# Two edits of order in the second input projection: the fifth normed tile and the sums of the second half

## The chip, the cores and the metric

The kernel runs on one core of one Trainium2 chip. The metric is the device time of one execution in microseconds (us), the median of a few runs. Weights and activations are float32; a product is made as three matmuls of a rounded part and its remainder (hi x hi, hi x lo, lo x hi), which is why TensorE is busy nearly all the time.

## The reference, cut to what matters

Two transformer blocks in a row, 1024 tokens, width 1024. Between them stand the places that the change touches:

```python
    # end of the first block
    gate = sigmoid(rmsnorm(h, ln3_g) @ w_ple_gate)
    h = h + gate * (p @ w_ple_proj)             # the "ple" stage
    h = rmsnorm(h, lnf_g)
    # start of the second block
    x = layer_norm(h, ln_in_g, ln_in_b)
    proj = x @ w_in_2                           # the second input projection, 22 column tiles of 128
```

The two norms are made as one: with d = lnf_g * h, the layer norm of the RMS norm needs the sum of d, the sum of d squared and the sum of h squared over the 1024 features of each token.

## The kernel before, in words

Data lie feature-major: tile k of h is 128 features (partitions) x 1024 tokens, k = 0 to 7. A half n is 512 tokens. All five engines run a list of instructions written out by hand; they meet at semaphores only, and each engine works through its own list in strict order, so an instruction that waits holds up everything behind it on that engine.

**The last four ple columns** are made as eight pieces, `PIECES` (line 83): pieces 0 to 3 are columns 4 to 7 of half 0, pieces 4 to 7 the same columns of half 1. PE's `piece` (line 1149) makes 24 matmuls for one. VectorE then does for each piece j: `piece_read` (line 2602, out of PSUM), `piece_gated` (2609, times the projected p, after ScalarE's sigmoid), `piece_added` (2616, into h), `piece_centre` (2622, d = lnf_g * h less a shift, after ScalarE has squared h), `sq1(j, 0)` and `sq1(j, 1)` (line 2678, which call `piece_square_in`, 2629: adding ScalarE's squares of h and of d). The plain sum of d is added by GpSimd's `piece_sum` (713) or, for pieces 3 and 7, by VectorE's `piece_sum_in` (2639).

**The norm of a half** goes: PE's `half_sums` (line 1179; 16 small matmuls, line 1175, that add over the partitions), VectorE's `half_variance` (2646; three small instructions), ScalarE's `half_root` (1850), VectorE's `half_inverse` (2655) and `half_factors` (2660), PE's `half_rows` (1210; 16 small matmuls, line 1217, that spread the two factors over the partitions into PSUM). VectorE's `normed` (2665) then makes each tile k of that half with a multiply (line 2672) and a subtraction (line 2676), both of SBUF with PSUM. ScalarE's `normed_hi` (1855) applies gain and offset (line 1858) and rounds to `B_hi` (line 1864); GpSimd's `normed_lo` (720) makes the remainder `B_lo` (line 726).

**The projection's first four columns** are made by PE's `quad` (line 1270). For a half n it loops over the eight tiles k, and for each k over four columns j, in four PSUM banks: eight matmuls from `B_hi` (lines 1259 and 1262) and four from `B_lo` (line 1266). It waits for `op_hi` of tile k ahead of the eight and for `op_lo` ahead of the four. What stands in the dictionary `before` is issued ahead of tile k and of its wait.

So `quad(0, ...)` runs on the normed tiles of half 0 while the last ple pieces of half 1 are still being finished on VectorE, and the sums and rows of half 1 are issued between its tiles.

**ScalarE's list** in this stretch (lines 1887 to 1893) stays as it is:

```python
            normed_hi(0, 0), piece_square(6, 0), normed_hi(1, 0), piece_gate(7)
            normed_hi(2, 0), piece_square(6, 1), normed_hi(3, 0), piece_square(7, 0), normed_hi(4, 0), piece_square(7, 1), normed_hi(5, 0)
            tick(act.activation(R[0:1, 0:1], col("one")[0:1, :], ACT.Sqrt))
            half_root(N1, 1, "ln_rms_eps")
            normed_hi(6, 0)
            tick(act.activation(R[0:1, 0:1], col("one")[0:1, :], ACT.Sigmoid))
            normed_hi(7, 0)
```

`piece_square(7, 0)` waits for `piece_added(7)`, `piece_square(7, 1)` for `piece_centre(7)`. `piece_centre(7)` overwrites h and waits for `piece_square(7, 0)`. GpSimd's list (lines 742 and 743) is `normed_lo` of tiles 0, 1 and 2, `piece_sum(6)`, `normed_lo` of tiles 3 to 7, and then the second half. It stays too.

Of the kernel before, what the change touches and what calls it, by code (L numbers as in the profile page):

```python
# [86 lines left out]
N1 = Norm(S_PLE, C_PLE, E3 + 2 * FULL, 2, FULL, 5, 0, 4, 0, 3, 2, 0)  # L87
# [97 lines left out]
def build(nc, x_t, p_t, weights, vec, w_gate_up, consts, masks, onehot, window, rel_bias, w_sp, rows, b_sp, bias_scratch,  # L185
          out):
    with ExitStack() as ctx:
# [8 lines left out]
        def at(name, kb, shape, dt=F32):  # L196
            return nc.alloc_sbuf_tensor_at(name, shape, dt, offset=base + int(kb * KB))
# [68 lines left out]
        acc2 = at("acc2", 40, [P, T])  # L266
# [122 lines left out]
        def hs(n):  # L389
            return slice(n * HT, (n + 1) * HT)  # L390
# [32 lines left out]
        def col(name, j=0):  # L423
            return vecs[:, bass.ds(VEC[name] + j, 1)]
# [32 lines left out]
        def quad(t, m, n):  # L457
            return t[:, m, n * HT:(n + 1) * HT]
# [360 lines left out]
        def _(pe):  # L819
# [352 lines left out]
            def sums_by_quarter(st, n, which, src, start=True, stop=True):  # L1172

                for g in range(4):
                    mm = pe.matmul(sums_of_half(st, n, which)[g * QP:(g + 1) * QP, :], ones[:, 0:QP], src[:, g * P:(g + 1) * P],
                                   start=start, stop=stop)
                return mm

            def half_sums(st, n, total, last=True):


                if n and st is N2:
                    pe.wait_ge(acc_free[1], (st.out + KT - 2) // 2 + 1)
                elif n == 0:
                    pe.wait_ge(pc_read, st.made + 3)
                pieces = 4 * n + (4 if last else 3)
                if not last:
                    pe.wait_ge(pc_read, st.made + 4)
                pe.wait_ge(sum_done, st.sq + st.per * pieces)
                pe.wait_ge(part_done, st.part + pieces)  # L1190
                sums_by_quarter(st, n, 0, acc[:, hs(n)], stop=last)
                mm = sums_by_quarter(st, n, 1, total[:, hs(n)], stop=last)
                if last:
                    mm.then_inc(stat_done, 1)
# [15 lines left out]
            def half_rows(st, n):  # L1210

                pe.wait_ge(hf_small, st.small + 5 * n + 5)
                banks_of = [(U[:, 2 + n, :], 2), (U[:, n, :], 0)]
                for dst, row in banks_of:
                    for g in range(4):
                        first = ident[:, g * QP:g * QP + 1].broadcast_to([P, P])
                        mm = pe.matmul(dst[:, g * P:(g + 1) * P], first, sm[:, n, row, :], start=True, stop=True)
                    mm.then_inc(rows_done, 1)
# [34 lines left out]
            def quad_hi(n, k, j):  # L1253

                if k == 0:
                    quad_free(n, j)
                wh, wl = (t[:, k * P:(k + 1) * P] for t in quad_w[j])
                x = B_hi[:, k, hs(n)]
                mm = pe.matmul(quad_bank[n][j], wh, x, start=(k == 0), stop=False)  # L1259
                if n == 0 and k == 0:  # L1260
                    mm.then_inc(w_used, 1)
                pe.matmul(quad_bank[n][j], wl, x, start=False, stop=False)

            def quad_lo(n, k, j):

                mm = pe.matmul(quad_bank[n][j], quad_w[j][0][:, k * P:(k + 1) * P], B_lo[:, k, hs(n)], start=False, stop=(k == KT - 1))
                if k == KT - 1:
                    mm.then_inc(acc_done if n else pc_made, 1)

            def quad(n, before):  # L1270

                for k in range(KT):
                    if k in before:
                        before[k]()
                    parts = ((0, 1, 2, 3),)
                    if n == 0 and k == 0:
                        parts = (0, 1, 2), (3,)
                    elif n and k == KT - 1:
                        parts = ((2, 3, 0, 1),)
                    pe.wait_ge(op_hi, 3 * KT + KT * n + k + 1)  # L1280
                    for part in parts:
                        for j in part:
                            quad_hi(n, k, j)
                        pe.wait_ge(op_lo, 3 * KT + KT * n + k + 1)
                        for j in part:
                            quad_lo(n, k, j)

            quad(0, {5: lambda: half_sums(N1, 1, acc2), 7: lambda: half_rows(N1, 1)})
            quad(1, {})
            gemm(0, S_IN2 + 4, a2 + 1, 1, B_hi, B_lo)  # L1290
            gemm(w3, S_IN2 + 5, a2 + 2, 0, B_hi, B_lo)
# [791 lines left out]
        def _(dve):  # L2083
# [186 lines left out]
            def normed(c):  # L2270
                dve.wait_ge(rt_done, c + 1)
                tick(dve.reciprocal(rs[:, :], rs[:, :]))
                tick.wait()
                dve.tensor_tensor(on[:, :, :], U[:, 2, :].rearrange("p (h n) -> p h n", h=GLA_H),
                                  rs[:, :].unsqueeze(2).broadcast_to([P, GLA_H, DV]), ALU.mult).then_inc(on_done, 1)
# [326 lines left out]
            def piece_read(j):  # L2602

                k, n = PIECES[j]
                g = 1 - k % 2
                dve.wait_ge(acc_done if n else pc_made, C_PLE + k + 1 if n else j + 1)
                dve.tensor_tensor(gs[:, k % 2, hs(n)], G[g][:, hs(n)], R[:, hs(n)], ALU.mult).then_inc(acc_free[g] if n else pc_read, 1)

            def piece_gated(j):

                k, n = PIECES[j]
                t = gs[:, k % 2, hs(n)]
                dve.wait_ge(sg2_done, FULL + j + 1)
                return tick(dve.tensor_tensor(t, t, pj[k % 2][:, k // 2, hs(n)], ALU.mult))

            def piece_added(j, product):

                k, n = PIECES[j]
                tick.wait(product)
                dve.tensor_tensor(h[:, k, hs(n)], h[:, k, hs(n)], gs[:, k % 2, hs(n)], ALU.add).then_inc(h_done, 1)  # L2620

            def piece_centre(j):

                k, n = PIECES[j]
                dve.wait_ge(h_done, FULL + j + 1)
                dve.wait_ge(sq_done, N1.sq + 2 * j + 1)
                dve.scalar_tensor_tensor(h[:, k, hs(n)], h[:, k, hs(n)], col("lnf", k), U[:, n, :], ALU.mult, ALU.subtract).then_inc(d_done, 1)

            def piece_square_in(st, j, e=0):

                k, n = PIECES[j]
                u = e if st.per == 2 else k % 2
                dve.wait_ge(sq_done, st.sq + st.per * j + e + 1)
                dve.wait_ge(sum_done, st.sq + st.per * j + e)
                last = (KT - 1, 1) if st.per == 2 else (KT - 1 - n, 0)
                dst = acc[:, hs(n)] if (k, e) == last else U[:, 2 + n, :]
                dve.tensor_tensor(dst, U[:, 2 + n, :], sq[:, u, hs(n)], ALU.add).then_inc(sum_done, 1)

            def piece_sum_in(st, j, total):

                k, n = PIECES[j]
                dve.wait_ge(d_done, st.d + j + 1)
                dve.wait_ge(part_done, st.part + j)
                dve.tensor_tensor(total[:, hs(n)], total[:, hs(n)], h[:, k, hs(n)], ALU.add).then_inc(part_done, 1)
# [33 lines left out]
            def sq1(j, e):  # L2678
                piece_square_in(N1, j, e)
# [20 lines left out]
            piece_added(5, p5), half_inverse(N1, 0), piece_centre(5), half_factors(N1, 0), sq1(5, 0), sq1(5, 1)  # L2700
            piece_read(6), normed(N1, 0, 0, 1)
            p6 = piece_gated(6)
            piece_added(6, p6), piece_read(7), normed(N1, 0, 2), piece_centre(6), normed(N1, 0, 3), sq1(6, 0)
            p7 = piece_gated(7)
            piece_added(7, p7), sq1(6, 1), normed(N1, 0, 4, 5), piece_centre(7), sq1(7, 0), piece_sum_in(N1, 7, acc2), sq1(7, 1)
            normed(N1, 0, 6)
            half_variance(N1, 1)
            normed(N1, 0, 7)
# [401 lines left out]
```

## Time and profile before

| | us |
|---|---|
| median of 3 runs | 1638.79 (1638.63 to 1638.92) |
| the profiled execution, its own time | 1638.46 |
| its span, first to last instruction | 1636.5 |
| PE busy in it | 1607.6 (98%) |
| VectorE (DVE) busy | 1145.8 (70%) |
| ScalarE (ACT) busy | 629.8 (38%) |
| GpSimd (POOL) busy | 709.7 (43%) |
| mean granted TensorE clock, of full | 0.999 |

A span starts with the first instruction and ends with the last; every time in a row is in us from its start, durations in us. A row of a timeline gives start, duration, engine, line, operation, output and inputs, their sizes and how many instructions are merged in it. Brackets at its end say how long the engine stood idle before it, and for whom. Records of neighbouring matmuls overlap: one takes 0.39 us from issue to its end while the next is issued 0.23 us after it. A group of merged instructions has the duration from the first start to the last end. The projection's `quad(0)` runs from 1193.36 to 1221.14, `quad(1)` from 1221.14 to 1242.88.

### The profile page before, as it was taken

How to read it: one execution, taken by the hardware profiler on the slowest of the kernel's cores; microseconds unless marked ns; L12 is line 12 of the kernel's file. 1: busy time of each engine (PE TensorE's matmuls, PEld its weight loads, DVE VectorE, ACT ScalarE, POOL GpSimd, SP SyncE). 2: the span in 40 equal slices, each digit the busy share in tenths (PEclk: the TensorE clock that was granted, in tenths of full speed). 3: DMA queues.
4: the chain of work that ended last, by engine and by line, in shares of the span. 5: the costliest groups of instructions: out<-in, count | busy, mean ns of one | idle time of the engine just before them, and what ended most of it. 6: DMA issues, size and time to landing. Idle time of an engine off the chain costs nothing.

```text
span 1636.5 us, 21082 instructions
## 1 busy us (share of the span) xinstructions
PE 1607.6 (98%) x7644; PEld 1306.5 (80%) x7644; DVE 1145.8 (70%) x1650; ACT 629.8 (38%) x1012; POOL 709.7 (43%) x390
## 2 busy tenths in 40 slices
PE   9999999999999999999999999999999999999997
PEld 5888888888877888888888778887878888877775
DVE  6342788863498777777767756886986994399557
ACT  6221444421265444444444222254562002268214
POOL 2435111155514333322326687762555554445452
PEclk9999999999999999999999999999999999999999
DMA  5511110141623443344449995322201111110012
GB/s 198 88 54 39 39 39 26 39 159 51 222 83 143 155 155 142 142 156 154 154 175 352 406 368 231 142 84 110 64 27 39 51 39 52 40 52 27 14 39 103
DMA packets 54566, 190.31 MB, mean 116 GB/s; under 512 B 5857, under 2 KB 7842, under 8 KB 53834
## 3 DMA queue, kind: packets, MB, share of 16 engines
q1 hardware_dynamic: 49362, 171.66, 28.9%
q10 hardware_dynamic: 5112, 17.44, 3.6%
q8 instruction: 56, 0.92, 0.2%
q14 instruction: 36, 0.29, 0.1%
HBM read 134.02 MB, written 55.05 MB: 116 GB/s over the span
## 4 chain that ended last, share of the span: by engine, by line
PE 54%; DVE 6%; DMA 3%; issue 2%; SPq 1%; ACT 1%; POOL 1%; ACTq 0%; DVEq 0%; POOLq 0%
PE G L825 16%; PE U L1092 11%; PE G L1092 10%; PE U L1130 4%; PE G L1130 4%; PE G L1166 4%; SPq L517 1%; DMA fraw<-in_weights 1%; PE U L1370 1%; PE G L1358 1%; DMA raw<-in_weights 1%; DMA hid_spill<-hst 1%; DVE h L2506 1%; DMA hid_spill<-hst_last 1%; PE G L1259 0%
## 5 line engine op out<-in xcount | busy, mean ns | idle before, releaser
L627 POOL TENSOR_SCALAR w_hi<-raw 128x1024 fp32r<-128x1024 f32 x48 | 143.0, 2980 | 276.9 <-PE G L825 213.5
L825 PE MATMUL G<-B_hi,w_hi 128*128 128x512 f32 x480 | 149.5, 393 | 0.2 <-ACT yb L1918 0.2
L825 PE MATMUL G<-B_lo,w_hi 128*128 128x512 f32 x480 | 147.9, 389 | 0.0
L825 PE MATMUL G<-B_hi,w_lo 128*128 128x512 f32 x480 | 147.8, 389 | 0.0
L671 POOL TENSOR_TENSOR S<-fraw 128x512 f32<-128x512 f32 x33 | 46.9, 1420 | 221.4 <-DVE ring_lo L2401 196.0
L825 PE MATMUL G<-A_hi,w_hi 128*128 128x512 f32 x432 | 138.3, 401 | 0.0
L825 PE MATMUL G<-A_lo,w_hi 128*128 128x512 f32 x432 | 133.5, 390 | 0.0
L825 PE MATMUL G<-A_hi,w_lo 128*128 128x512 f32 x432 | 133.3, 390 | 0.0
L629 POOL TENSOR_TENSOR w_lo<-raw,w_hi 128x1024 fp32r<-128x1024 f32 x48 | 127.6, 2658 | 4.0
L1092 PE MATMUL G<-X_lo,ring_hi 128*128 128x512 f32 x308 | 120.3, 390 | 2.3 <-DVE X_lo L2396 2.3
L1092 PE MATMUL G<-X_hi,ring_hi 128*128 128x512 f32 x308 | 120.1, 390 | 1.7 <-DVE ring_lo L2401 1.2
L1644 ACT ACTIVATE ring_hi<-S 128x512 fp32r<-128x512 f32 x132 | 82.0, 628 | 103.1 <-PE U L1130 48.0
L1092 PE MATMUL U<-X_hi,ring_hi 128*128 128x512 f32 x308 | 120.2, 390 | 0.3 <-DVE ring_lo L2401 0.3
L1092 PE MATMUL G<-X_hi,ring_lo 128*128 128x512 f32 x308 | 119.9, 389 | 0.0
L1092 PE MATMUL U<-X_hi,ring_lo 128*128 128x512 f32 x308 | 119.8, 389 | 0.0
L1092 PE MATMUL U<-X_lo,ring_hi 128*128 128x512 f32 x308 | 119.8, 389 | 0.0
L1644 ACT ACTIVATE ring_hi<-fraw 128x512 fp32r<-128x512 f32 x99 | 61.5, 627 | 123.0 <-PE U L1130 60.5
L825 PEld LDWEIGHTS G<-B_hi,w_hi 128*128 128x128 f32 x480 | 89.7, 188 | 20.5 <-issue 2.5
L825 PEld LDWEIGHTS G<-B_lo,w_hi 128*128 128x128 f32 x480 | 90.1, 188 | 18.9
L825 PEld LDWEIGHTS G<-B_hi,w_lo 128*128 128x128 f32 x480 | 90.1, 188 | 18.8
L2731 DVE SCALAR_TENSOR_TENSOR co<-yb,vecs,co 128x1009 f32<-128x1009 f32 (+14 forms) x60 | 95.5, 1667 | 0.0
L825 PEld LDWEIGHTS G<-A_hi,w_lo 128*128 128x128 f32 x432 | 81.1, 188 | 17.4
(436 smaller groups left out, 3814.1 us busy)
## 6 DMA issues: line engine op xcount, KB each, us to landing
raw<-in_weights SPq DMA_DIRECT2D x72, 512.0 KB, 3.6
hid_spill<-hst SPq DMA_DIRECT2D x72, 512.0 KB, 2.6
fraw<-in_weights SPq DMA_DIRECT2D x66, 512.0 KB, 4.5
Dc<-hid_spill SPq DMA_DIRECT2D x56, 512.0 KB, 12.7
Dc<-hid_spill ACTq DMA_DIRECT2D x14, 512.0 KB, 7.8
h<-in_x_t SPq DMA_DIRECT2D x8, 512.0 KB, 7.9
h_spill<-h SPq DMA_DIRECT2D x8, 512.0 KB, 6.6
pj_spill<-pj_out SPq DMA_DIRECT2D x8, 512.0 KB, 2.7
```

Source lines behind the costliest of these rows:

```text
L517: sp.dma_start(f(Dc[c % 2][:, r, n, :, :].rearrange("p a n -> p (a n)")), hid_spill[2 * c + n, :, r, :]).then_inc(ch_in[c % 2][r], 16)
L627: pool.tensor_scalar(hi, raw[:, u, :], 1.0, None, ALU.mult).then_inc(w_hi_done, 1)
L629: pool.tensor_tensor(lo, raw[:, u, :], f(hi), ALU.subtract).then_inc(w_split, 1)
L671: pool.tensor_tensor(s1, a21, a22, ALU.add).then_inc(s_sum, 1)
L825: mm = pe.matmul(G[g][:, b * HT:(b + 1) * HT], w, x[:, k, b * HT:(b + 1) * HT], start=s0, stop=s1)
L1092: mm = pe.matmul(banks[x][BANK_OF[r]], a, b[r][:, k, :], start=(r < 4 and k == 0 and n == 0), stop=(k == 3 and n == 2), skip_group_check=( ...
L1130: mm = pe.matmul(banks[m][BANK_OF[r]], a, b, start=(r < 4 and n == pairs[0] and e == 0), stop=(n == pairs[-1] and e == 2), skip_group_chec ...
L1166: mm = pe.matmul(G[g][:, hs(n)], a, x[:, kk, hs(n)], start=(kk == 0 and e == 0), stop=(kk == KT - 1 and e == 2))
L1358: mm = pe.transpose(G[0][:, e % 2 * HT + kb * P:e % 2 * HT + (kb + 1) * P], scores_of(n, par, head(e))[:, kb * P:(kb + 1) * P], ident[:, :])
L1370: mm = pe.matmul(U[HD * g:HD * g + HD, 2 + par, 2 * half * P:2 * (half + 1) * P].rearrange("p (j n) -> p j n", j=2), Vt[:, kb0 + kb, HD * ...
L1644: act.activation(ring(ring_hi, w, r), combo(w, r), ACT.Copy).then_inc(f_hi[w % 2], 1)
L2731: tick(dve.scalar_tensor_tensor(co[:, j, lo:hi], yb[:, j, lo + o:hi + o], w, co[:, j, lo:hi], ALU.mult, ALU.add))
```

## The change

Three lines change. On PE, the sums of the second half are issued ahead of tile 6 of `quad(0)` and not ahead of tile 5. On VectorE, the normed tile 4 of half 0 is made before `piece_gated(7)`, and not after `sq1(6, 1)` together with tile 5. The normed tile 5 comes after `piece_centre(7)` and not before it. No instruction is added or taken away, except that tiles 4 and 5, which shared one pass of `normed` (two multiplies, two subtractions), have one each.

```diff
-            quad(0, {5: lambda: half_sums(N1, 1, acc2), 7: lambda: half_rows(N1, 1)})
+            quad(0, {6: lambda: half_sums(N1, 1, acc2), 7: lambda: half_rows(N1, 1)})
...
-            piece_added(6, p6), piece_read(7), normed(N1, 0, 2), piece_centre(6), normed(N1, 0, 3), sq1(6, 0)
+            piece_added(6, p6), piece_read(7), normed(N1, 0, 2), piece_centre(6), normed(N1, 0, 3), sq1(6, 0), normed(N1, 0, 4)
             p7 = piece_gated(7)
-            piece_added(7, p7), sq1(6, 1), normed(N1, 0, 4, 5), piece_centre(7), sq1(7, 0), piece_sum_in(N1, 7, acc2), sq1(7, 1)
+            piece_added(7, p7), sq1(6, 1), piece_centre(7), normed(N1, 0, 5), sq1(7, 0), piece_sum_in(N1, 7, acc2), sq1(7, 1)
             normed(N1, 0, 6)
             half_variance(N1, 1)
             normed(N1, 0, 7)
```

## Rows read from the trace of the kernel before

**Rows 1.** The page's part 1, the line of PE.

```profile
PE 1607.6 (98%) x7644; PEld 1306.5 (80%) x7644; DVE 1145.8 (70%) x1650; ACT 629.8 (38%) x1012; POOL 709.7 (43%) x390
```

**Rows 2.** Busy time in the stretch of quad(0): stretch, PE, PEld, DVE, ACT, POOL, clock.

```profile
1193.36:1221.14 27.78, 25.84 (x130) 19.72 (x128) 24.28 (x34) 17.43 (x27) 12.91 (x10) 1.00 0.07 20
```

**Rows 3.** Who PE waited for, whole span: total us, times, longest.

```profile
PE G L1259 <- ACT B_hi L1864: 1.6, 2, 1.2
```

**Rows 4.** Timeline of PE in quad(0), from tile 3 to the start of quad(1).

```profile
1203.11 0.39 PE L1259 MATMUL G<-B_hi,w_hi 128*128 128x512 f32 x1
...
1204.92 1.07 PE L1266 MATMUL G<-B_lo,w_hi 128*128 128x512 f32 x4
1207.16 0.50 PE L1259 MATMUL G<-B_hi,w_hi 128*128 128x512 f32 x1 [1.17 <-ACT B_hi L1864]
...
1209.11 1.07 PE L1266 MATMUL G<-B_lo,w_hi 128*128 128x512 f32 x4
1210.10 0.64 PE L1175 MATMUL U<-acc,ones 128*32 128x128 f32 x16
...
1213.73 0.50 PE L1259 MATMUL G<-B_hi,w_hi 128*128 128x512 f32 x1
...
1216.60 1.95 PE L1217 MATMUL U<-sm,ident 128*128 128x128 f32 x16
...
1221.14 0.39 PE L1259 MATMUL U<-B_hi,w_hi 128*128 128x512 f32 x1
```

**Rows 5.** Timeline of ACT: piece_square(7, 0), normed_hi(4), piece_square(7, 1), half_root, normed_hi(6).

```profile
1203.05 0.63 ACT L1848 ACTIVATE sq<-h 128x512 f32<-128x512 f32 x1 [1.76 <-DVE h L2620]
1205.63 0.81 ACT L1858 ACTIVATE h<-h,vecs 128x512 f32<-128x512 f32 x1 [1.95 <-DVE h L2676]
1206.48 0.63 ACT L1864 ACTIVATE B_hi<-h 128x512 fp32r<-128x512 f32 x1
1207.02 0.61 ACT L1848 ACTIVATE sq<-h 128x512 f32<-128x512 f32 x1
...
1211.90 0.41 ACT L1853 ACTIVATE sm<-sm,vecs 128x128 f32<-128x128 f32 x1 [1.39 <-DVE sm L2653]
1212.21 0.80 ACT L1858 ACTIVATE h<-h,vecs 128x512 f32<-128x512 f32 x1
```

**Rows 6.** Timeline of DVE, from piece_gated(7) to the first instruction of half_variance.

```profile
1200.02 1.30 DVE L2614 TENSOR_TENSOR gs<-gs,pj 128x512 f32<-128x512 f32 x1
1201.35 1.66 DVE L2620 TENSOR_TENSOR h<-h,gs 128x512 f32<-128x512 f32 x1
...
1203.54 1.27 DVE L2672 TENSOR_TENSOR h<-h,U 128x512 f32<-128x512 f32 x2
...
1206.11 0.74 DVE L2627 SCALAR_TENSOR_TENSOR h<-h,vecs,U 128x512 f32<-128x512 f32 x1
...
1208.95 0.68 DVE L2637 TENSOR_TENSOR acc<-U,sq 128x512 f32<-128x512 f32 x1
1209.55 0.67 DVE L2672 TENSOR_TENSOR h<-h,U 128x512 f32<-128x512 f32 x1
1210.33 0.69 DVE L2676 TENSOR_TENSOR h<-h,U 128x512 f32<-128x512 f32 x1
1210.93 0.28 DVE L2649 TENSOR_SCALAR sm<-U 128x128 f32<-128x128 f32 x1
```

**Rows 7.** Timeline of POOL beside them: B_lo of tile 2, piece_sum(6), B_lo of tile 3.

```profile
1199.47 1.29 POOL L726 TENSOR_TENSOR B_lo<-h,B_hi 128x512 fp32r<-128x512 f32 x1 [0.59 <-ACT B_hi L1864]
1200.72 1.74 POOL L718 TENSOR_TENSOR acc<-acc,h 128x512 f32<-128x512 f32 x1
1202.42 1.74 POOL L726 TENSOR_TENSOR B_lo<-h,B_hi 128x512 fp32r<-128x512 f32 x1
```

**Rows 8.** PE's last matmuls of the kernel, from its timeline.

```profile
1625.62 2.05 PE L1452 MATMUL U<-sm,ident 128*128 128x128 f32 x16
```

**Rows 9.** Busy times of one later stretch, columns as in rows 2.

```profile
1632.00:1633.00 1.00, 0.00 (x0) 0.00 (x0) 0.83 (x2) 1.00 (x2) 0.00 (x0) 0.61 0.90 334
```

## The prediction

> **What bounds the kernel now.** The page's part 1 comes first: PE is busy for 98% of the span [rows 1]. A change of order can win back only PE's idle time, and it costs wherever it makes more of that. The stretch of `quad(0)` says how much there is here: 27.78 us long with PE busy for 25.84, so 1.94 us idle [rows 2]. The table of waits puts 1.2 us of it on one wait, for ScalarE's `B_hi` [rows 3]. PE's timeline shows where that is, at tile 4 [rows 4]. Twelve matmuls make a tile. They are issued 0.227 us apart (1203.11 to 1204.92 is eight of them), so an undisturbed tile takes 2.72 us. Tile 3 is through at 1204.92 + 4 x 0.227 = 1205.83, and tile 4 starts at 1207.16: 1.33 us lost. Tile 4, restarting from idle, takes 1.95 + 0.91 = 2.86. The sums follow at 1210.10, then tile 5, and tile 6 starts at 1213.73.
>
> ScalarE's timeline says what tile 6 waits on [rows 5]. `half_root` starts at 1211.90 after 1.39 us of idling for VectorE's variance. Only then comes `normed_hi(6)` at 1212.21; a normed tile on ScalarE takes 1.48 us from its start to the end of `B_hi` (1205.63 to 1206.48 + 0.63 = 1207.11). So `B_hi` of tile 6 is there at 1213.69, and PE starts on it at 1213.73. From the start of the sums to the start of tile 6 is a chain of 3.63 us, PE to VectorE to ScalarE to PE. Today tile 5 is made inside it, and it costs next to nothing.
>
> **The change, part by part.** Nothing is computed more or less, and no DMA is issued by any moved step, so SP's queue is untouched. GpSimd's list stays in its order.
>
> *Tile 4 before `piece_gated(7)`.* A tile normed alone takes VectorE 1.47 us from the multiply to the end of the subtraction (1209.55 to 1210.33 + 0.69) [rows 6]. It would start where `piece_gated(7)` does now, at 1200.02, and end at 1201.49. `piece_gated(7)` and `piece_added(7)` come later by about 1.4. Both read only SBUF, and their lengths, 1.30 and 1.66 us against 0.67 to 0.69 for their neighbours with a PSUM operand, end each about 0.55 us after a GpSimd instruction: 1201.32 after 1200.76, 1203.01 after 1202.46 [rows 6, 7]. GpSimd's 1.74 us likewise hold about 0.45 of waiting, since the first of its rows takes 1.29. I take them as excluding each other. Then `piece_sum(6)`, now with no SBUF-only instruction against it, runs 1200.72 to 1202.01; `piece_gated(7)` ends at 1202.56; `B_lo` of tile 3 at about 1203.71; `piece_added(7)` at 1204.26 instead of 1203.01.
>
> That matters, because ScalarE's list has `piece_square(7, 0)` ahead of `normed_hi(4)`, and it waits for `piece_added(7)`. The normed tile 4 is there at 1201.49 and lies waiting. The square starts at 1204.30 (0.04 behind its input, as 1203.05 is behind 1203.01), ScalarE's next instruction 0.53 later, and `B_hi` is done 1.48 after that: 1206.31, PE at 1206.35 [rows 5]. **Gain at tile 4: 0.8 us of the 1.33.** Bounds: if neither VectorE instruction met GpSimd (0.7 each), `piece_added(7)` would end at 1202.9 and the whole 1.33 be won, and with it the 0.14 of the restart; if GpSimd went first once more (another 0.4), the gain would be 0.4. I take 0.8, since in each such meeting of [rows 6, 7] the one that waited went next.
>
> *Tile 5 after `piece_centre(7)`.* `piece_centre(7)` waits for that square (end 1204.93) and can start at 1205.05, where now it starts at 1206.11. Behind it tile 5: 0.66 + 1.47, normed at 1207.18. ScalarE has `piece_square(7, 1)` out of the way by then, so `B_hi` of tile 5 is done at 1208.70. PE wants it at 1206.35 + 2.86 = 1209.21: hidden, with 0.5 us to spare. Should that cover go, each 0.1 us costs 0.1.
>
> *The inputs of the sums.* From `piece_centre(7)` to the last of them is 3.52 us now (1206.11 to 1208.95 + 0.68), and one normed tile, 1.4, is put in between: 1205.05 + 3.52 + 1.4 = 1210.0 at the latest. PE reaches the sums, behind tile 5, at 1209.21 + 2.72 = 1211.93. They are not late. They would have been so ahead of tile 5 by up to 0.8 us, so moving them protects tile 5.
>
> *The sums behind tile 5.* This is the dear part. The chain sums, `half_variance`, `half_root`, `normed_hi(6)`, tile 6 stays as it is, but tile 5 is no longer inside it. It took 3.63 us; about 0.1 of that was VectorE ending `normed(6)` (1210.33 + 0.69 = 1211.02) when the sums had ended at 1210.74, and that falls away, since VectorE is then idle from about 1211.4. So 3.5 us, of which PE works 0.64: tile 6 starts at 1211.93 + 0.08 + 3.5 = 1215.5, with PE idle for 2.9 us ahead of it. **Against 1213.73 that is 1.8 us later.** From there all moves together: tile 6 takes 2.87 (1213.73 to 1216.60), and the rows and tile 7 take 4.54 (1216.60 to 1221.14) [rows 4]. Queued behind the waiting `half_root` are `normed_hi(6)` and (7) on ScalarE; behind the waiting `half_variance` are tile 7, the inverse and the factors on VectorE. PE takes the factors at 1216.60 now, 6.5 us after the start of the sums at 1210.10; then it would be 1218.4, again 6.4 us after them. So that wait opens by 0.1 at most, and tile 7, which PE takes 1.7 us later still, does not open at all. GpSimd's remainders wait only for ScalarE and stay 1.3 us behind it, inside the eight matmuls of a tile (1.81).
>
> *Sum.* From the start of tile 4 to that of tile 6 PE now takes 6.57 us (1207.16 to 1213.73): tile 4, 2.86, a gap of 0.08, and the chain, 3.63. After the change it is tile 4, 2.86, tile 5, 2.72, the gap, and the chain of 3.5: 9.16. That is 2.6 more, and 0.8 was won ahead of it: **+1.8 us**. PE is the bound of the rest, so the start of `quad(1)` and the end move by as much. The profiled execution took 1638.46, which makes 1640.3; the median of the runs lies 0.33 above it, so I forecast 1638.79 + 1.8 = **1640.6**. With the bounds at tile 4 (+1.1 and +2.2) its own range is 1639.9 to 1641.0.
>
> *TensorE's clock.* A new idle of 2.9 us is longer than the 1.2 of [rows 3]. The last matmul of the kernel ends at 1627.67 [rows 8]. The granted clock is full until the stretch from 1632 to 1633, whose 0.61 is 0.22 at full and 0.78 at half, so it fell at about 1632.2 [rows 9]: 4.5 us of idling without a fall. By that, 2.9 us cost nothing beyond themselves. The Trainium skill ("TensorE: Matmul & The Clock Gate", "A second HAM failure mode: psum-queue depth-cycling") says that even short pauses between groups of matmuls can let the clock swing between its two levels; here there would be three pauses within 25 us. Its result is the first rival.
>
> **The rivals.**
> - *The clock falls* to 1.2 GHz after the new pause (ends on the other side: slower). One tile at half speed takes 5.44 instead of 2.72 us, so +1.8 + 2.7: 1643.3. It decides if the granted clock behind the pause reads half. Against it: the 4.5 us above and the full clock through all of `quad(0)` [rows 2]. This is the cited page's rule at work. Chance 0.06.
> - *The early tile 4 brings nothing*: `B_hi` of tile 4 stays behind `piece_square(7, 0)` and comes no earlier than 1207.1. For it: ScalarE's list, and the two SBUF-only instructions. Then tile 5 ends at 1210.02 + 2.72 = 1212.74, tile 6 starts at 1216.3: +2.6, 1641.4. Chance 0.07.
> - *The sums' chain is hidden* all the same, and the move does what one would wish: tile 6 right behind the sums, at 1211.93 + 0.08 + 0.64 = 1212.65, 1.1 us earlier than now, 1637.7. Against it: `normed_hi(6)` stands behind `half_root` in ScalarE's list [rows 5]. Chance 0.05.
> - *It is taken up later*: a wait further on is shortened by as much, 1638.8. Against it: the waits still to come also hang on PE's own products. Chance 0.06.
>
> My forecast has the remaining 0.76.
>
> **How the numbers follow.** A measurement of this kernel tells about 0.2%, or 3.3 us, from no change. Only the clock rival lies beyond that, with a little for what I have not seen; nothing lies beyond on the fast side, where all that `quad(0)` idles is 1.94 us. So faster 0.02, same 0.91, slower 0.07. The range takes the forecast with its bounds, the rival without a gain and the one that is taken up later, with the runs' scatter of 0.3: 1638.7 to 1642.0. It leaves out the clock and the hidden chain.
>
> **What would show it right or wrong.** In the changed profile: tile 4 of `quad(0)` some 0.8 us earlier, after an idle of about 0.4 waiting for `B_hi`; no idle ahead of tile 5; the 16 sums at 1212.0; then PE idle for 2.9 us and released by `B_hi`, with `half_root` ahead of it idling for VectorE's variance; `piece_added(7)` ending at 1204.3; `quad(1)` at 1222.9 (1221.14 + 1.8) and the granted clock full throughout. The prediction is wrong if PE goes from the sums into tile 6 at once, if tile 4 is not earlier, or if `quad(1)` starts at 1222.9 and the end does not follow.

## The result, and the profile after

The median rose from 1638.54 us to 1642.08 us (19 runs of each, the changed kernel from 1640.19 to 1644.9, the kernel before from 1637.23 to 1639.34). The ratio is 1.002 with a 95% interval of 1.0014 to 1.0027: slower by 2.3 to 4.4 us, and the scatter of the runs has doubled. The profiled execution is the third shortest of the changed kernel's 19: 1640.62 us, span 1638.6, against 1638.46 and 1636.5. So there are two things to explain: what this one trace shows, 2.1 us, and why most executions lie another 1 to 2 us above it.

First the trace. The stretches of `quad(0)`, of `quad(1)` and of all the rest, from the busy times of the changed kernel (columns as in [rows 2]):

```profile
1193.80:1223.41 29.61, 25.63 (x130) 19.80 (x128) 23.44 (x34) 17.42 (x27) 12.46 (x10) 1.00 0.06 19
1223.41:1245.15 21.74, 21.74 (x97) 17.84 (x95) 7.23 (x12) 11.42 (x19) 15.27 (x10) 1.00 0.09 25
1245.15:1638.60 393.45, 378.29 (x1955) 301.73 (x1954) 288.69 (x407) 131.55 (x276) 189.77 (x81) 0.99 0.15 46
```

`quad(0)` takes 29.61 us where it took 27.78 [rows 2]: +1.83. `quad(1)` takes the 21.74 it took before (1221.14 to 1242.88), and what follows 393.45 against 393.62 before, so nothing is given back later. The row of the kernel before for that rest:

```profile
1242.88:1636.50 393.62, 378.37 (x1955) 301.70 (x1954) 288.92 (x407) 131.62 (x276) 189.85 (x81) 0.99 0.15 46
```

In the changed kernel the stretch begins at 1193.80 instead of 1193.36, ahead of anything that changed. That start moves between 1192.9 and 1194.4 from one profile to the next in the runs below and is scatter of the 1190 us before it. Times are therefore compared from the start of `quad(0)`; in this trace, take 0.44 off.

PE's timeline of the changed kernel, against [rows 4]:

```profile
1206.80 0.50 PE L1259 MATMUL G<-B_hi,w_hi 128*128 128x512 f32 x1 [0.35 <-ACT B_hi L1864]
...
1211.47 1.07 PE L1266 MATMUL G<-B_lo,w_hi 128*128 128x512 f32 x4
1212.47 0.64 PE L1175 MATMUL U<-acc,ones 128*32 128x128 f32 x16
1215.97 0.50 PE L1259 MATMUL G<-B_hi,w_hi 128*128 128x512 f32 x1 [2.86 <-ACT B_hi L1864]
...
1218.87 1.95 PE L1217 MATMUL U<-sm,ident 128*128 128x128 f32 x16
```

With 0.44 taken off, tile 4 starts at 1206.36 (1207.16 before), tile 6 at 1215.53 (1213.73 before), behind a pause of 2.86 us. The table of waits has the same wait as [rows 3], grown by 2.0 us:

```profile
PE G L1259 <- ACT B_hi L1864: 3.6, 3, 2.9
```

ScalarE's timeline, against [rows 5], says what that pause waits for:

```profile
1204.75 0.63 ACT L1848 ACTIVATE sq<-h 128x512 f32<-128x512 f32 x1 [3.02 <-DVE h L2620]
1205.28 0.80 ACT L1858 ACTIVATE h<-h,vecs 128x512 f32<-128x512 f32 x1
1206.12 0.63 ACT L1864 ACTIVATE B_hi<-h 128x512 fp32r<-128x512 f32 x1
...
1214.15 0.40 ACT L1853 ACTIVATE sm<-sm,vecs 128x128 f32<-128x128 f32 x1 [3.51 <-DVE sm L2653]
1214.46 0.80 ACT L1858 ACTIVATE h<-h,vecs 128x512 f32<-128x512 f32 x1
```

`half_root` idles for 3.51 us where it idled for 1.39, and `normed_hi(6)` is queued behind it. VectorE, against [rows 6], and GpSimd, against [rows 7], show the other half, tile 4's part:

```profile
1201.84 1.17 DVE L2614 TENSOR_TENSOR gs<-gs,pj 128x512 f32<-128x512 f32 x1
1203.05 1.66 DVE L2620 TENSOR_TENSOR h<-h,gs 128x512 f32<-128x512 f32 x1
...
1213.18 0.29 DVE L2649 TENSOR_SCALAR sm<-U 128x128 f32<-128x128 f32 x1 [2.38 <-PE U L1175]
```

```profile
1201.16 1.31 POOL L718 TENSOR_TENSOR acc<-acc,h 128x512 f32<-128x512 f32 x1
1202.42 1.74 POOL L726 TENSOR_TENSOR B_lo<-h,B_hi 128x512 fp32r<-128x512 f32 x1
```

`piece_gated(7)` ends at 1203.01, 0.54 behind the end of GpSimd's sum (1202.47), and `piece_added(7)` at 1204.71, 0.55 behind the end of its `B_lo` (1204.16). That is the same pattern as before the change. ScalarE's square starts 0.04 behind it.

### The profile page after: what moved, and what is told of

The parts are those of the page before. It is cut to its first block, busy times and chain, and to the rows that moved or that the text cites. A ratio compares the mean times of both kernels' runs of the same rounds, so it can differ in the third digit from the quotient of the medians.

```text
span 1638.6 us, 21083 instructions
## 1 busy us (share of the span) xinstructions
PE 1607.4 (98%) x7644; PEld 1306.6 (80%) x7644; DVE 1144.6 (70%) x1650; ACT 629.8 (38%) x1012; POOL 709.2 (43%) x390
## 4 chain that ended last, share of the span: by engine, by line
PE 54%; DVE 6%; DMA 3%; issue 3%; ACT 1%; SPq 1%; POOL 1%; ACTq 0%; DVEq 0%; POOLq 0%
PE G L825 16%; PE U L1092 11%; PE G L1092 10%; PE U L1130 4%; PE G L1130 4%; PE G L1166 4%; SPq L517 1%; DMA fraw<-in_weights 1%; DMA raw<-in_weights 1%; DMA hid_spill<-hst 1%; PE U L1370 1%; PE G L1358 1%; DMA hid_spill<-hst_last 1%; DVE h L2506 1%; PE G L1259 0%
## 5 line engine op out<-in xcount | busy, mean ns | idle before, releaser
L2506 DVE TENSOR_TENSOR h<-h,G 128x512 f32<-128x512 f32 x108 | 71.7, 682 | 33.4 <-PE G L1130 27.6
```

Of the source, the lines that this page charges most:

```text
L2506: dve.tensor_tensor(q, q, banks[m][BANK_OF[r]], ALU.add).then_inc(dn_ev[m], 1)
```

## Experiments

**1. The changed kernel once more, and with its pause filled.** The trace above has the full clock up to 1634.7 us, 4.8 us after its last matmul. The other executions have mean granted clocks of 0.998 or less more often, one has 0.996 at 1643.47 us and one 0.947 at 1644.9 (a value that nothing here explains). That is thin evidence, as the kernel before shows 0.998 too, and a mean moves by as much with the moment at which the clock falls behind the last matmul (the last kernel of experiment 6 reads 0.998 with a full clock up to 1629.6); so a control, and a kernel in which PE is busy during the pause without coming to tile 6 any sooner:

```diff
+            def sums_and_fill():
+                half_sums(N1, 1, acc2)
+                for _ in range(11):
+                    pe.matmul(U[:, 1, :], w3[0][:, 0:P], B_hi[:, 0, 0:HT], start=True, stop=True)
-            quad(0, {6: lambda: half_sums(N1, 1, acc2), 7: lambda: half_rows(N1, 1)})
+            quad(0, {6: sums_and_fill, 7: lambda: half_rows(N1, 1)})
```

> The changed kernel once more, as the control of this group. Its trace put tile 6 of quad(0) 1.8 us later against the start of quad(0), but its median came out 3.5 us above the kernel before. Theory A (the pause of 2.86 us ahead of tile 6 is all there is): the median is 1.8 us above the kernel before, 1640.4 or so, and the runs agree as closely as those of the kernel before (within about 1 us). Theory B (in many executions TensorE's granted clock falls behind the pause and costs 1 to 3 us more): the median is 3 to 4 us above, 1642, the runs spread from +1.7 to +6 us, and the longer a run is, the lower its mean granted clock (0.998 and less where the kernel before has 0.999).

> The changed kernel, with 11 idle-time matmuls (128x512, into a free bank, nobody reads them) put behind the sums of the second half, where PE pauses for 2.86 us. At 0.227 us each they take 2.5 us, so PE's pause shrinks to 0.3 to 0.4 us but tile 6 still starts at the same time, as its operand does not come sooner. Theory A: nothing changes, the same median as the changed kernel beside it (within 0.4 us). Theory B: the clock no longer falls, the runs close up to within 1 us of each other, and the median drops to 1.8 us above the kernel before, 1.5 to 2 us below the changed kernel.

Measured on one chip, 11 runs of each and 30 of the kernel before (1638.88): the control 1642.21 (1640.68 to 1643.59), ratio 1.0021 (1.0011 to 1.003); filled 1640.96 (1639.02 to 1642.13), ratio 1.0012 (1.0003 to 1.0021). Filling takes 1.25 us off the median and leaves +2.1; in 106 of the 121 pairs of one run of each, the control's is the longer. The runs did not close up to within 1 us, as theory B had it: the filled ones spread over 3.1 us and the control's over 2.9. The profiled execution of the control was a middling one this time, and shows what the first trace could not. PE's timeline:

```profile
1212.40 0.64 PE L1175 MATMUL U<-acc,ones 128*32 128x128 f32 x16
1215.91 0.50 PE L1259 MATMUL G<-B_hi,w_hi 128*128 128x512 f32 x1 [2.87 <-ACT B_hi L1864]
...
1216.98 0.63 PE L1262 MATMUL G<-B_hi,w_lo 128*128 128x512 f32 x1
1217.41 0.63 PE L1259 MATMUL G<-B_hi,w_hi 128*128 128x512 f32 x1
...
1220.35 1.95 PE L1217 MATMUL U<-sm,ident 128*128 128x128 f32 x16
```

and its busy times in halves of a microsecond (the number before the last two is the granted clock):

```profile
1216.00:1216.50 0.50, 0.50 (x2) 0.41 (x3) 0.47 (x2) 0.50 (x1) 0.50 (x1) 0.87 0.00 0
1216.50:1217.00 0.50, 0.50 (x3) 0.34 (x2) 0.50 (x1) 0.50 (x1) 0.50 (x1) 0.50 0.00 0
...
1219.50:1220.00 0.50, 0.50 (x3) 0.41 (x2) 0.00 (x0) 0.00 (x0) 0.50 (x1) 0.72 0.00 0
```

PE is back at work at 1215.91. The clock falls to half, 1.2 GHz, at 1216.37 (0.87 is 0.74 of the half microsecond at full), 3.3 us after the sums ended at 1213.04, and is back at 2.4 GHz at 1219.78. In between the matmuls are issued 0.43 us apart and not 0.23. From the start of tile 6 to the rows it takes 4.44 us against 2.90 in the trace without a fall: 1.54 us more. `quad(0)` takes 31.18.

In the filled kernel the pause is gone, tile 6 starts no sooner, and the clock stays full; `quad(0)` takes 29.57 us. PE's timeline there, the unused matmuls on line 1292:

```profile
1212.65 0.65 PE L1175 MATMUL U<-acc,ones 128*32 128x128 f32 x16
1213.22 2.83 PE L1292 MATMUL U<-B_hi,w_hi 128*128 128x512 f32 x11
1216.17 0.50 PE L1259 MATMUL G<-B_hi,w_hi 128*128 128x512 f32 x1
```

So theory A, the pause alone, holds for some executions (the first trace), and theory B for others (the control's): a fall of the clock behind the pause. That theory B holds for most executions is read from the medians and not from traces: the control's lies 3.3 us above the kernel before, 1.5 more than the 1.8 of the first trace.

**2. Each half of the change alone.** The kernel before with PE's line only, and the changed kernel with PE's line put back.

```diff
-            quad(0, {5: lambda: half_sums(N1, 1, acc2), 7: lambda: half_rows(N1, 1)})
+            quad(0, {6: lambda: half_sums(N1, 1, acc2), 7: lambda: half_rows(N1, 1)})
```

> The kernel before, with only PE's sums of the second half moved behind tile 5 (one line). Tile 4 keeps its wait of 1.33 us, the chain of 3.5 us lies bare: tile 6 starts 2.6 us later against the start of quad(0) than in the kernel before. Theory A: median +2.6 us, runs within 1 us. Theory B: the same pause of 2.9 us ahead of tile 6, and a longer one ahead of tile 4 than in the changed kernel, so +4 us or more, with scatter and clocks of 0.998 and less.

Measured beside the two above: 1643.67 us (1641.84 to 1645.2, 8 runs), +4.8 us, ratio 1.0031 (1.002 to 1.0041). Its profiled execution was the shortest of its runs, with a full clock in `quad(0)`; the stretch of `quad(0)` is 2.64 us longer than before:

```profile
1194.06:1224.48 30.42, 25.65 (x130) 19.79 (x128) 24.37 (x34) 17.42 (x27) 12.93 (x10) 1.00 0.06 18
```

> The changed kernel's order on VectorE, with PE's sums back ahead of tile 5. Tile 4 starts 0.8 us earlier than before; the sums' inputs are ready at about 1209.0 against the 1209.3 at which PE comes (counted from the start of quad(0) as before); VectorE ends normed(6) at 1210.3, so the variance starts 0.7 us earlier than before, and tile 6 too. Both theories: -0.7 us, 1637.9, no pause over 1 us, runs as close as those of the kernel before. If the inputs of the sums are late instead (what moving the sums was to avoid), PE idles ahead of tile 5 and the gain shrinks to 0.3 us or less.

Measured: 1638.08 us (1637.58 to 1639.43, 11 runs), -0.8 us against 1638.88, ratio 0.9995 (0.9986 to 1.0004), so not told from no change by its interval, though in the trace `quad(0)` takes 27.09 us (1193.57 to 1220.66), 0.69 less than before. The sums are not late: PE's timeline has no idle ahead of them.

```profile
1209.51 0.65 PE L1175 MATMUL U<-acc,ones 128*32 128x128 f32 x16
1210.08 0.50 PE L1259 MATMUL G<-B_hi,w_hi 128*128 128x512 f32 x1
...
1213.27 0.50 PE L1259 MATMUL G<-B_hi,w_hi 128*128 128x512 f32 x1
```

Here tile 5 ends at 1212.06 + 0.91 = 1212.97 and tile 6 starts 0.3 us later, so the chain of the sums takes back a little of what tile 4 won; behind the moved sums the norms bring 0.81 (2.64 to 1.83). All of the loss is PE's one line.

**3. What lays the chain bare: ScalarE's queue.** The changed kernel with `normed_hi(6)` ahead of the root. The added `tick.wait()` stands in for the same wait inside `normed_hi(6)`, which has moved away with it.

```diff
+            normed_hi(6, 0)
             tick(act.activation(R[0:1, 0:1], col("one")[0:1, :], ACT.Sqrt))
             half_root(N1, 1, "ln_rms_eps")
-            normed_hi(6, 0)
+            tick.wait()
             tick(act.activation(R[0:1, 0:1], col("one")[0:1, :], ACT.Sigmoid))
```

> The changed kernel, with normed_hi(6) taken out of the queue behind half_root on ScalarE (it now comes ahead of the table switch and the root). If that queue is what lays the sums' chain bare, tile 6 starts right behind the sums, 1.1 us earlier than in the kernel before (counted from the start of quad(0)) and 2.9 us earlier than in the changed kernel; the rows ahead of tile 7 then wait for the factors by 0.8 us, and the time is 0.3 us below the kernel before, 1638.5, with no pause over 1 us, no fall of the clock, and the scatter gone. Rival (the chain is bare for another reason, VectorE's or GpSimd's): the pause ahead of tile 6 stays over 2 us and the time at +1.8 us or more.

Measured: 1638.47 us (1637.66 to 1640.25, 11 runs) against 1638.79 (33 runs), ratio 1.0 (0.9991 to 1.0009), 0.3 below as expected, but well inside the interval. `quad(0)` takes 27.61 us, 2.0 less than in the changed kernel. The pause ahead of tile 6 is gone, and a smaller one stands ahead of the rows, for the factors:

```profile
1211.91 0.65 PE L1175 MATMUL U<-acc,ones 128*32 128x128 f32 x16
1214.46 1.08 PE L1266 MATMUL G<-B_lo,w_hi 128*128 128x512 f32 x4
1216.19 2.05 PE L1217 MATMUL U<-sm,ident 128*128 128x128 f32 x16 [0.65 <-DVE sm L2664]
```

So the pause was made by the place of `normed_hi(6)` in ScalarE's list, and by nothing in the data: its input had been ready since 1210.81 in the changed kernel's trace, where VectorE's subtraction for tile 6 is

```profile
1210.12 0.69 DVE L2676 TENSOR_TENSOR h<-h,U 128x512 f32<-128x512 f32 x1
```

**4. How long a pause it takes.** The filled kernel with 5 and with 2 of the unused matmuls instead of 11.

> The changed kernel with 5 of the unused matmuls behind the sums: they take 1.1 us of the 2.86 us, so PE pauses for 1.7 us and tile 6 starts as late as in the changed kernel. If only a pause near 3 us lets the clock fall, this kernel equals the one with 11 (+2.1 us against the kernel before); if a shorter one does too, it lies between that and the changed kernel's +3.4, and some runs are 1.5 us above the others.

> The changed kernel with 2 unused matmuls behind the sums, so PE pauses for 2.2 to 2.4 us and not 2.86. If the fall of the clock needs nearly the whole pause, the median is that of the kernels with 5 and 11 of them, +2.1 us against the kernel before; if its frequency shrinks with the pause, it lies between, +2.5 to +3.

The first matmul of tile 6 with 5 of them, and with 2:

```profile
1216.51 0.50 PE L1259 MATMUL G<-B_hi,w_hi 128*128 128x512 f32 x1 [1.49 <-ACT B_hi L1870]
```

```profile
1216.43 0.50 PE L1259 MATMUL G<-B_hi,w_hi 128*128 128x512 f32 x1 [2.20 <-ACT B_hi L1870]
```

With 5, PE pauses for 1.49 us: 1640.95 us (1639.38 to 1641.93) against 1638.79, +2.2, the same as with 11. With 2, it pauses for 2.20 us: 1642.53 (1639.98 to 1643.36) against 1638.59, +3.9, the same as the changed kernel or a little more. The trace with 2 has a fall, though its pause is 0.66 us shorter (busy times, clock as before):

```profile
1216.00:1220.00 4.00, 3.57 (x10) 2.86 (x11) 1.85 (x2) 3.19 (x5) 1.96 (x2) 0.68 0.00 0
1220.00:1221.00 1.00, 1.00 (x5) 0.78 (x4) 0.00 (x0) 0.00 (x0) 0.61 (x1) 0.59 0.00 0
```

At half from 1217.4 to 1220.8, again 3.4 us, though PE had worked since 1216.43; `quad(0)` takes 31.21. Neither of the two outcomes I had expected (+2.1, or +2.5 to +3) came: the excess did not shrink with the pause.

The runs' mean clocks agree. Of the 51 executions with a pause of 2.2 or 2.9 us (those of experiment 5 included) 11 have 0.997 or less; of the 161 without (the kernel before in these comparisons, the kernels filled with 5 and 11, and those of experiments 2, 3 and 6 that have no such pause) none has.

**5. Two more profiles**, one each, of the changed kernel and of the one with the sums alone.

> The changed kernel, one more profile. Of its 30 runs so far some 5 lie within 0.5 us of the lowest and the rest 1 us or more above. So most likely (4 in 5) the trace shows the granted clock at half for some 3 us behind the pause ahead of tile 6, and quad(0) takes 30.5 to 31.5 us; otherwise it is full throughout and quad(0) takes 29.6.

> The kernel with the sums alone moved, one more profile. Its first showed no fall and was the fastest of its 8 runs. Most likely (4 in 5) this one shows the clock at half behind the pause, quad(0) in 31.5 to 32.5 us; otherwise 30.4.

The changed kernel took 1643.37 us and `quad(0)` 32.44, more than the 30.5 to 31.5 expected. This time the clock falls while PE still pauses and stays down twice as long, from 1215.27 to 1222.1 (busy times):

```profile
1215.00:1215.50 0.50, 0.00 (x0) 0.00 (x0) 0.50 (x2) 0.47 (x2) 0.00 (x0) 0.77 0.00 0
...
1216.00:1222.00 6.00, 6.00 (x16) 4.89 (x17) 1.32 (x2) 2.69 (x4) 2.49 (x2) 0.50 0.00 0
1222.00:1222.50 0.50, 0.50 (x6) 0.50 (x5) 0.00 (x0) 0.00 (x0) 0.00 (x0) 0.90 0.00 0
```

That costs 32.44 - 29.61 = 2.8 us. The other took 1642.28 us, `quad(0)` 31.97, at half from 1216.75 to 1220.16: 1.55 us more than its trace with a full clock. Three traces of the changed kernel thus have the three cases, no fall, 3.4 us and 6.8 us at half, with 29.61, 31.18 and 32.44 us for the same stretch of work.

**6. Toward a kernel better than both.** First ScalarE's and VectorE's lists brought in line with the sums behind tile 5: `normed_hi(4)` ahead of `piece_square(7, 0)`, the table switch and `normed_hi(6)` and (7) ahead of `half_root`, `normed(N1, 0, 7)` ahead of `half_variance`.

> The changed kernel, with the queues brought in line with it: on ScalarE normed_hi(4) ahead of piece_square(7, 0), the switch of tables ahead of normed_hi(6), and (6) and (7) ahead of half_root; on VectorE normed(7) ahead of half_variance. Tile 4 then has no wait (1.3 us won), tile 5 at most 0.2, tile 6 follows the sums at once, the factors come 0.3 us after PE asks: quad(1) starts 1.4 us earlier than in the kernel before against the start of quad(0), so 1.4 us below it, without scatter. If piece_square(7, 0) or the chain of the factors turns out later than worked out, PE idles ahead of tile 5 or of the rows and the gain is 0.5 to 1.

Measured: 1637.91 us (1636.54 to 1640.05) against 1638.79, ratio 0.9995 (0.9986 to 1.0005). `quad(0)` takes 26.82 us, 0.96 less than before and not 1.4: the factors come 0.3 us after PE could take them. One of the small instructions of `half_variance`, both operands in SBUF, took 0.63 us instead of 0.29, which is 0.34 of the 0.44 that are missing; why it did was not tried.

The other way keeps the sums where they were. With the change's order on VectorE and `normed_hi(6)` ahead of the root, as in experiment 3:

> VectorE's part of the change with the sums back ahead of tile 5, and normed_hi(6) ahead of half_root. Tile 4 0.8 us earlier as in the kernel with the norms only, and the 0.3 us that tile 6 still waits there gone too: 1.0 us below the kernel before. If the root, now 0.7 us later, delays the rows ahead of tile 7 instead, it stays at -0.7.

Measured: 1637.69 us (1637.05 to 1639.14) against 1638.79, ratio 0.9996 (0.9987 to 1.0005), `quad(0)` 26.68. And with one more pair of ScalarE's list exchanged:

```diff
-            ... normed_hi(3, 0), piece_square(7, 0), normed_hi(4, 0), piece_square(7, 1), ...
+            ... normed_hi(3, 0), normed_hi(4, 0), piece_square(7, 0), piece_square(7, 1), ...
```

> The kernel with the norms, normed_hi(6) ahead of the root and the sums ahead of tile 5 (26.7 us for quad(0), 1.1 below the kernel before), with normed_hi(4) also ahead of piece_square(7, 0) on ScalarE. Tile 4 then has no wait; PE comes to the sums 0.45 us before their inputs. Net 0.3 us more: quad(0) in 26.4 us, the time 1.4 us below the kernel before. If piece_square(7, 0) is put off by normed_hi(4), the inputs of the sums slip and the gain stays at 1.1 or less.

Measured: 1637.31 us (1636.99 to 1638.05, 11 runs) against 1638.59 (1637.52 to 1639.55, 21 runs), -1.3 us. The interval of the ratio, 0.9993 (0.9984 to 1.0002), just takes in 1; the trace has `quad(0)` in 26.36 us, 1.42 less than before, with tile 4 no longer waiting and 0.31 us of waiting ahead of the sums:

```profile
1193.73:1220.09 26.36, 25.29 (x130) 19.82 (x129) 22.71 (x34) 17.65 (x27) 12.90 (x10) 1.00 0.07 21
```

```profile
1209.40 0.64 PE L1175 MATMUL U<-acc,ones 128*32 128x128 f32 x16 [0.31 <-DVE acc L2638]
```

It has the lowest median of all kernels here, and the closest of all groups of 8 runs or more.

## Why the prediction was right, and where not

*Tile 4.* Forecast 0.8 us earlier, with `B_hi` held by `piece_square(7, 0)` and that by two instructions excluded by GpSimd's. Measured 0.80 (1207.16 to 1206.36). The last experiment shows that queue directly: with `normed_hi(4)` ahead of the square, tile 4 does not wait at all.

*Tile 5, and the inputs of the sums.* Forecast hidden and in time. Right: PE idles ahead of neither. But "moving them protects tile 5" was wrong: with the sums left in place (experiment 2) their inputs were not late either. My bound of 1210.0 for these inputs had counted one addition, `piece_sum_in(7)`, at the 1.66 us that it took before; it took 0.68, and they were ready at 1208.97, 0.24 ahead of the 1209.21 at which PE, by the forecast, is through with tile 4.

*The sums behind tile 5.* Forecast a chain of 3.5 us laid bare, a pause of 2.9, +2.6 for this edit alone and +1.8 for both. Measured 3.50 (1212.47 to 1215.97), 2.86, +2.64 and +1.83. What shows the queue is experiment 3: 2.0 us back for moving one step of ScalarE's list.

*Later.* Forecast that all of it reaches the end. Right: the rest takes 393.45 us against 393.62.

*TensorE's clock.* This is the step that failed: "By that, 2.9 us cost nothing beyond themselves", with a chance of 0.06 for the rival. By the medians it happens in most executions; in the profiles it did in two of three of the changed kernel. Where the same kernel has a trace without a fall beside it, the fall costs 1.5 to 1.6 us twice and 2.8 once, and 1.8 + 1.5 = 3.3 is the control's excess over the kernel before (1642.21 less 1638.88), against the forecast 1.8. The measured median, 1642.08, is 1.5 above the forecast of 1640.6 and stands 0.08 above the top of the range; the range had left that rival out. (That the median comes so close to the top is no merit of the terms: the forecast's largest, the rival without a gain at 1641.4 with the scatter of 0.3, give 1641.7 and not 1642.0.) Against the kernel before measured beside it the excess is 3.5 us, about twice the 1.8 forecast. It is also beyond the 3.3 us that the prediction held for the smallest change to be told from none: with 19 runs of each, the interval is only 1 us to either side. My ground had been the end of the kernel, where the clock held for 4.5 us after the last matmul [rows 8, 9]. One stretch of idling was read as a bound that holds every time. It does not hold even for that place: in the fourteen traces of these kernels the clock fell from 2.5 to 5.3 us after the end of the last matmul. The shortest is in experiment 5's profile of the changed kernel, whose last matmul ends at 1632.62 and whose clock falls at 1635.1 (0.56 is 0.12 at full):

```profile
1630.57 2.05 PE L1452 MATMUL U<-sm,ident 128*128 128x128 f32 x16
```

```profile
1635.00:1636.00 1.00, 0.00 (x0) 0.00 (x0) 1.00 (x3) 1.00 (x2) 0.86 (x2) 0.56 0.99 367
```

Behind the pause ahead of tile 6 the same clock fell 2.2 to 3.6 us after the start of a pause and as late as 1.0 us after PE had resumed, or not at all. The rival's own price, 2.7 us, was also of the wrong size for the common case: it took a whole tile's 2.72 us of work at half speed, where half speed covered 3.4 us and made the stretch 1.5 to 1.6 us longer.

In the profiles, pauses of 2.2 and 2.9 us ahead of tile 6 were followed by a fall in four traces of six. No shorter pause was, in any of the fourteen traces and anywhere between the first matmul and the last; the longest of these is 1.54 us. The Trainium skill ("TensorE: Matmul & The Clock Gate", "A second HAM failure mode: psum-queue depth-cycling") says that short pauses between groups of matmuls can make the clock swing between its levels; for the pauses of 2.2 and 2.9 us the traces agree, and the chance of 0.06 that I had given to it was too little; for the shorter pauses of this kernel no trace shows it.

## What to carry to other kernels

Before a step is moved behind the work that hid it, look at who is queued behind each wait of its chain on the other engines: here one instruction in ScalarE's list, ready long before, turned a chain of 3.5 us into a pause of PE. A pause of PE can be dearer than it is long, as those of 2.2 and 2.9 us were here, and a single trace may not show it. What did show it was a median 1.5 us above the profiled execution, and runs with a mean clock of 0.997 and less. The spread of a few runs did not: it was 3.1 us with the pause filled, 3.5 in the first kernel of experiment 6, which has no pause there, and 2.9 in the control. One profile, and above all one of the shortest, is a sample: where the median lies above the profiled execution by more than it did before, profile again.

## What was not expected of the hardware

The granted clock fell after PE had resumed work: 0.5, 0.8 and 1.0 us after, in three of the four traces with a fall, and 0.6 us before it did in the fourth. It stayed at half for 3.4 us in three of them and 6.8 in one, though PE worked all the while after the pause. Pauses of 1.54 us and less never showed it in the profiles, and the medians with 1.49 us and with none agree within 0.1 us of each other against their kernels before (+2.2 and +2.1). What decides whether a given execution falls was not tried and stays open. So does a rest of 0.3 us by which the filled kernels lie above the +1.8 of their traces, within the intervals, and one of 0.6 us by which the kernel with the sums alone (+4.8) lies above the 2.64 of its full-clock trace and the 1.55 of a fall.
